# Fewer key pairs in the expert choice, paired low parts in scoring, twelve more row halves moved there, spread loads and a reordered end

## The chip, the cores and the metric

The kernel runs on one core of a Trainium2 chip. The metric is device time in microseconds (us) of one launch, median of 3 runs. The core has a matrix engine (TensorE, PE in the profile, with PEld for its weight loads), a vector engine (VectorE, DVE), a scalar engine (ScalarE, ACT), a third elementwise engine that also issues gathers (GpSimd, POOL) and a queue for loads (SyncE, SP). Each runs its own list of instructions in order; they meet only at semaphores.

## The reference

One layer over 256 tokens of width 2048, in float32:

```python
hn = rmsnorm(x); q, k, v, u, z = split(hn @ w_in)          # 2048 x 5120
x = x + concat(diff_attention(q, k, v), gmlp(u, z)) @ w_out  # 2048 x 2048
xb = rmsnorm(x)
q = (xb @ w_q).reshape(T, 8, 2, 128)                        # 8 heads, two halves
sc = einsum('thcd,hckd->thck', q, sub_keys)                 # 128 keys a half
s1, i1 = top_k(sc[:, :, 0], 16); s2, i2 = top_k(sc[:, :, 1], 16)
best, ci = top_k((s1[..., :, None] + s2[..., None, :]).reshape(T, 8, 256), 16)
idx = 128 * i1[ci // 16] + i2[ci % 16]                      # 16 of 16384 experts
act = gelu(einsum('td,thkd->thk', xb, u_tab[idx]))
x = x + einsum('thk,thkd->td', softmax(best) * act, v_tab[idx])
out = rmsnorm(x)
```

top_k returns its values in falling order. So pair (a, b) has (a+1)(b+1)-1 pairs that are at least as large, and only pairs with (a+1)(b+1) <= 16 can be among the best 16.

## The kernel before, in words

**Stages.** Input projection, attention and gating, output projection, query projection (32 units of `wq_t`), then three stages that the change touches:

- *Scoring* of all 16384 experts for 200 of the tokens: 128 steps `j`, two units a step, `n = 2j` and `2j+1`, from the table `u_t` (512 KB a unit, ring of 6).
- *Values*: 256 units `v` from `peer_v` (512 KB each, ring of 10).
- The *end*: transposes back, residual, final norm, stores.

The other 56 tokens are done by gathering their chosen rows ("halves of rows"): 232 halves of 128x1024 floats (512 KB), each gathered by POOL into one of 3 buffers `PICKED` and used by DVE (`half_rows`: a dot product with x for rows of `peer_u`, L1263, or a multiply-add into an accumulator for rows of `peer_v`, L1271). `HALF_STEPS` says in which scoring steps they are used, `HALF_UNITS` in which units of values. POOL gathers half k when DVE has used half k-3.

**Two-part arithmetic.** Every weight unit is split in a high part that ACT makes (`top(n)`, L737, ring `HI` of 4) and a low part, raw minus high, that DVE makes (`low(n)`, L1205) or, in a few scoring steps, POOL (`by_pool`, L493). In values DVE makes two low parts with one instruction (`low_pair`, L1198).

**Order in scoring.** PE, for unit n: 8 high products of unit n (L1652), then 8 low products of unit n-1 (L1658). DVE in step j: `sum_halves(j)` (waits for PE's low products of unit 2j+1 and for ACT's copy), `low(2j+4)`, `low(2j+5)`, pieces of the choice, `apply_gates`, `one_hots`, `land`, then halves of rows. ACT in step j: `low_half_out(j)` (copies half of the PE result, L762), `top(2j+5)`, `gelu(j)`, `top(2j+6)`, `put_gates`, `gates_into(j+2-SPREAD0)` (waits for DVE's `one_hots` of the same step, L783). From step 37 (`SPREAD0`) to 86 the gates of 4 tokens a step are spread to experts: DVE compares (`one_hots`, L1224), ACT scales (`gates_into`), PE multiplies (`spread`, L1636), DVE and ACT apply.

**The choice** (top 16 of keys, of pairs, and decoding) is a generator of 41 pieces for each of two token tiles. `EARLY` pieces of each tile run in the query stage; `piece_steps` puts the others into scoring steps 1 to 32 by a table of costs and an allowance for each step. A top 16 is five DVE instructions (L1110 to L1114). PE transposes the result of a tile in steps 18 and 34 (L1643). A piece on key half c waits for ACT's copy number c//2+1 of the key scores; in ACT's list copies 1 to 6 stand in the query stage and copy 7 behind the first four `top` of scoring.

**Other loads.** POOL loads `X8` (x rows for the last 24 gathered tokens, five pieces of 192 KB) in one go beside gather 99, and the residual and final gain (twelve pieces of 256 KB) one behind each gather from unit 178 on.

Of the kernel before, what the change touches and what calls it, by code (L numbers as in the profile page):

```python
# [14 lines left out]
P = 128  # L15
T, D = 256, 2048
# [23 lines left out]
RING = 6  # L40
# [31 lines left out]

TILE_ORDER = (1, 0)
EARLY = 12
QUERY_BESIDE = range(WQ0 + 11, WQ_END, 2)
CHOICE0 = 1

def piece_cost(i):  # L80

    if i < HC:
        return 1.55
    if HC + 2 <= i < HC + 2 + PH:
        return 2.35
    return 0.5 if i in (HC + 2 + PH, HC + 2 + PH + 7) else 1.4

def piece_steps():

    steps, j, room = [], CHOICE0, 0.0
    left = [i for o in range(2) for i in range(EARLY, PIECES)]
    while left:
        room += 2.6
        if left[0] in PLAIN and (len(left) < 2 or left[1] in PLAIN):
            room += 0.8
        while left and piece_cost(left[0]) <= room + 0.4:
            room -= piece_cost(left.pop(0))
            steps.append(j)
        j += 1  # L100
    n = PIECES - EARLY
    return [-1] * EARLY + steps[:n] + [-1] * EARLY + steps[n:]
# [5 lines left out]
              for j in range(NKEYS)}  # L108
# [9 lines left out]

HALVES = 4 * NG  # L120
HALF_STEPS = sorted([j for j in range(SPREAD0 - 3, SPREAD_END) if j % 3] + list(range(SPREAD_END, NKEYS - 7))
                    + list(range(SPREAD_END, NKEYS - 7, 4)))
FREE_UNITS = [u for u in range(9, 250) if u not in (NKEYS - 2, NKEYS - 1)]
HALF_UNITS = [FREE_UNITS[i * len(FREE_UNITS) // (HALVES - len(HALF_STEPS))] for i in range(HALVES - len(HALF_STEPS))]
A_DOTS, A_SUMS = 2 * GROUPS_A, 4 * GROUPS_A
B_DOTS, B_SUMS = A_SUMS + 2 * GROUPS_B, A_SUMS + 4 * GROUPS_B
# [8 lines left out]
    return k < B_DOTS, GROUPS_A + (k - A_SUMS) % (2 * GROUPS_B) // 2, k % 2  # L135

X8_AT = len(HALF_STEPS) + 20
SEL_A_AT = 2 * NKEYS - 4
GATHERED = {j: (ROW_SLOTS if j >= ROWS_BACK_AT else 0) + sum(i < j for i in HALF_STEPS) for j in range(NKEYS)}  # L140
S_BANKS = 3
# [24 lines left out]
def hybrid_peer_block(nc, x, w_in, w_out, wq_t, keys_t, u_t, peer_u, peer_v, ws_t, bs_t, gain_t, ffn_gain, z_gain,  # L166
                      final_gain, lambdas, rope, out):
    ctx = ExitStack()
    with ctx:  # L169
# [29 lines left out]

        SC = at("SC", 44 * KB, [P, TT, HC, NKEYS])  # L200
        QTQ = at("QTQ", 60 * KB, [P, HC, T])
        CAND = at("CAND", 60 * KB, [P, PH, TOPK, TOPK])
        EQ = at("EQ", 68 * KB, [P, PH, TOPK, TOPK])
        S16 = at("S16", 84 * KB, [P, TT, HC, TOPK])
        I16 = at("I16", 86 * KB, [P, TT, HC, TOPK], U32)
        I16F = at("I16F", 88 * KB, [P, TT, HC, TOPK])
# [212 lines left out]
        def _(pool):  # L419
# [114 lines left out]
                     for c in range(D // BANK)]  # L534
            for k in range(len(HALF_STEPS) + ROW_SLOTS, HALVES):
                gather(k)
                if k == X8_AT:
                    for r in range(ROWS_B):
                        pool.dma_start(X8[r * NB_:(r + 1) * NB_, :], xg_dram[NA:NS, :]).then_inc(x8_ready, 16)
                if HALF_UNITS[k - ROW_SLOTS - len(HALF_STEPS)] >= NKEYS + 50 and late:  # L540
                    pool.wait_ge(low_used, N_U + NKEYS + 44)
                    dst, src, done = late.pop(0)
                    pool.dma_start(dst, src).then_inc(done, 16)
            assert not late
            pool.wait_ge(fg_ready, 16 * D // BANK)
            for tt in range(TT):
                pool.wait_ge(sums, 7 + 2 * tt + 1)  # L547
                nc.gpsimd.tensor_tensor(X1R[:, tt, 0:HALF], X1R[:, tt, 0:HALF], FG[:, 0:HALF], ALU.mult).then_inc(gained, 1)  # L548

        @block.scalar
        def _(act):
# [297 lines left out]
            def final_scale(tt, cols):  # L850
                act.wait_ge(scaled, tt + 1)
                act.wait_ge(gained, tt + 1)  # L852
                nc.scalar.activation(X1R[:, tt, cols], X1R[:, tt, cols], ACT.Copy, scale=SS[:, 8 + tt:9 + tt])\  # L853
                    .then_inc(act_scaled, 1)

            act.wait_ge(fg_ready, 16 * D // BANK)
# [1 line left out]
            final_squares(0, 1)  # L858
            root(8, SS[:, 6:7])
            final_squares(1, 0)  # L860
            final_squares(1, 1)
# [7 lines left out]
        def _(dve):  # L869
# [246 lines left out]
            def choice(o):  # L1116

                tt = TILE_ORDER[o]
                for c in range(HC):
                    dve.wait_ge(sc_out, c // 2 + 1)  # L1120
                    top16(SC[:, tt, c, :], S16[:, tt, c, :], I16[:, tt, c, :])
                    yield
                dve.wait_ge(sc_out, HC // 2)
                link(v.tensor_copy(I16F[:, tt], I16[:, tt]))
                s1, s2 = S16[:, tt, 0:HC:2, :], S16[:, tt, 1:HC:2, :]
                lists = I16F[:, tt, 0:HC:2, :], I16F[:, tt, 1:HC:2, :]
                heads = [slice(0, PH // 2), slice(PH // 2, PH)]
                for hs in heads:
                    link(v.tensor_tensor(CAND[:, hs], s1[:, hs].unsqueeze(3).broadcast_to(grid),
                                         s2[:, hs].unsqueeze(2).broadcast_to(grid), ALU.add))  # L1130
                    yield
                for h in range(PH):
                    top16(CAND[:, h].rearrange("p a b -> p (a b)"), BEST[:, h], CI[:, h])
# [207 lines left out]
            def add_out(c, tt, count):  # L1341
# [459 lines left out]
```

## Time and profile before

| | us |
|---|---|
| median of 3 runs (lowest, highest) | 1769.67 (1769.17, 1772.12) |
| the profiled execution's own time | 1784.21 |
| its span | 1782.4 |
| PE busy | 1726.1 (97%) |
| DVE busy | 1443.7 (81%) |
| ACT busy | 987.6 (55%) |
| POOL busy | 425.3 (24%) |
| moved by DMA | 483.79 MB, 271 GB/s in the mean |

The profiled execution is 14.5 us longer than the median of the plain ones. Scoring runs from about 458 us to 1122 us of the span, values from there to 1767 us.
### The profile page before, as it was taken

The numbers are of one execution on the slowest core, as the hardware profiler recorded it, in microseconds if no ns is written. First come the engines' busy times: TensorE is split into PE (matmuls) and PEld (weight loads), VectorE is DVE, ScalarE is ACT, GpSimd is POOL, SyncE is SP. The second block draws the span as 40 slices with busy tenths as digits, with TensorE's granted clock in tenths as the row PEclk, the third lists the DMA queues.
The fourth block names the chain that finished last, engine by engine and source line by source line (L and its number), as shares of the span: only waits on it lengthen the run. The fifth ranks groups of instructions, "written<-read, shape, count | busy, mean of one in ns | idle before, by whom it ended". The sixth has DMA issues, their size and how long they took to land. (4 is left out here: it accounts for less than half of the span.)

```text
span 1782.4 us, 28846 instructions
## 1 busy us (share of the span) xinstructions
PE 1726.1 (97%) x10934; PEld 1639.2 (92%) x10934; DVE 1443.7 (81%) x2029; ACT 987.6 (55%) x1600; POOL 425.3 (24%) x324
## 2 busy tenths in 40 slices
PE   8999999999999999999999999997999999999997
PEld 7887778788998899999999999997999989999997
DVE  4546786578799988888989998676998889978996
ACT  5444574444554567777775555554455545554554
POOL 0002300034222001110114454034432323243221
PEclk9999999999999999999999999999999999999999
DMA  7665455676677577777779999899899989999993
GB/s 232 213 186 164 143 156 176 190 258 203 207 225 244 188 238 250 259 249 244 242 242 340 357 370 349 242 351 303 318 366 356 364 307 365 365 358 390 362 362 123
DMA packets 132855, 483.79 MB, mean 271 GB/s; under 512 B 15368, under 2 KB 15522, under 8 KB 132048
## 3 DMA queue, kind: packets, MB, share of 16 engines
q1 hardware_dynamic: 95760, 347.65, 59.3%
q0 software_dynamic: 36672, 133.77, 20.6%
q8 instruction: 87, 1.43, 0.3%
q10 hardware_dynamic: 288, 0.55, 0.1%
q14 instruction: 48, 0.39, 0.1%
HBM read 476.71 MB, written 5.20 MB: 270 GB/s over the span
## 5 line engine op out<-in xcount | busy, mean ns | idle before, releaser
L1692 PE MATMUL PS<-W,HI 128*128 128x400 f32 x2048 | 429.3, 351 | 25.1 <-DVE W L1282 21.5
L737 ACT ACTIVATE HI<-V_RAW 128x1024 fp32r<-128x1024 f32 x256 | 271.5, 1061 | 304.0 <-PE PS L1692 123.4
L1652 PE MATMUL PS<-xT,HI 128*128 128x400 f32 x2048 | 424.4, 349 | 0.1
L1692 PEld LDWEIGHTS PS<-W,HI 128*128 128x128 f32 x2048 | 362.4, 191 | 28.5 <-issue 22.6
L1652 PEld LDWEIGHTS PS<-xT,HI 128*128 128x128 f32 x2048 | 358.0, 190 | 3.0 <-ACT HI L737 1.2
L1198 DVE TENSOR_TENSOR V_LO<-V_RAW,HI 128x2048 fp32r<-128x2048 f32 x128 | 292.8, 2287 | 21.5 <-ACT HI L737 21.2
L737 ACT ACTIVATE HI<-RING_RAW 128x1024 fp32r<-128x1024 f32 x256 | 269.1, 1051 | 64.6 <-DMA RING_RAW<-u_t 59.7
L1205 DVE TENSOR_TENSOR RING_LO<-RING_RAW,HI 128x1024 fp32r<-128x1024 f32 x248 | 292.4, 1218 | 3.2 <-ACT HI L737 3.1
L1658 PEld LDWEIGHTS PS<-xT,RING_LO 128*128 128x128 f32 x2048 | 265.2, 191 | 9.5 <-DVE RING_LO L1205 9.4
L1658 PE MATMUL PS<-xT,RING_LO 128*128 128x200 f32 x2048 | 266.6, 273 | 6.2 <-DVE RING_LO L1205 6.0
L502 POOL DMA_INDIRECT PICKED<-peer_u,PK x116 | 144.1, 1243 | 531.5 <-DVE DOTS L1263 518.8
L1697 PEld LDWEIGHTS PS<-W,V_LO 128*128 128x128 f32 x2048 | 270.0, 192 | 0.0
L1697 PE MATMUL PS<-W,V_LO 128*128 128x200 f32 x2048 | 269.0, 273 | 0.0
L881 DVE TENSOR_TENSOR LO<-RAW,HI 128x1024 fp32r<-128x1024 f32 x121 | 149.4, 1237 | 123.5 <-PE PS L1404 97.6
L502 POOL DMA_INDIRECT PICKED<-peer_v,PK x116 | 167.0, 1439 | 324.0 <-DVE ACC L1271 240.8
L555 ACT ACTIVATE HI<-RAW 128x1024 fp32r<-128x1024 f32 x144 | 152.7, 1065 | 161.8 <-DMA RAW<-wq_t 46.4
L1271 DVE SCALAR_TENSOR_TENSOR ACC<-PICKED,DOTS,ACC 128x1024 f32<-128x1024 f32 (+1 forms) x112 | 143.3, 1281 | 56.4 <-DMA PICKED<-peer_v,PK 55.8
L1263 DVE CUSTOM_DVE_ANT_0 PICKED<-PICKED,X 128x1024 f32<-128x1024 f32 (+1 forms) x116 | 141.2, 1222 | 24.5 <-DMA PICKED<-peer_u,PK 24.2
L1397 PE MATMUL PS<-HI,xT 128*128 128x512 f32 x440 | 139.5, 398 | 2.0 <-ACT xT L580 1.3
L1404 PE MATMUL PS<-HI,xT 128*128 128x512 f32 x440 | 136.2, 391 | 0.6 <-DVE xT L900 0.6
L1404 PEld LDWEIGHTS PS<-HI,xT 128*128 128x128 f32 x440 | 82.5, 188 | 18.4 <-DVE xT L900 1.0
L1397 PEld LDWEIGHTS PS<-HI,xT 128*128 128x128 f32 x440 | 79.7, 188 | 17.2 <-ACT xT L580 1.5
(213 smaller groups left out, 1640.7 us busy)
## 6 DMA issues: line engine op xcount, KB each, us to landing
RING_RAW<-u_t SPq DMA_DIRECT2D x256, 512.0 KB, 4.8
V_RAW<-peer_v SPq DMA_DIRECT2D x256, 512.0 KB, 10.1
RAW<-w_in SPq DMA_DIRECT2D x80, 512.0 KB, 3.8
RAW<-w_out SPq DMA_DIRECT2D x32, 512.0 KB, 4.5
RAW<-wq_t SPq DMA_DIRECT2D x32, 512.0 KB, 4.8
x_spill<-X POOLq DMA_DIRECT2D x2, 1024.0 KB, 5.8
X1R<-x_spill POOLq DMA_DIRECT2D x8, 256.0 KB, 9.4
PICKED<-peer_u,PK POOLq DMA_INDIRECT x116, 8.1
```

The costliest lines, as they stand in the source:

```text
L502: pool.indirect_dma_start(PICKED[k % ROW_SLOTS][:], None, table.rearrange("e (a c) -> (e a) c", a=2), bass.IndirectOffsetOnAxis(PK4[:, hal ...
L555: nc.scalar.activation(HI[:, slot, :], RAW[:, slot, :], ACT.Copy).then_inc(hi_ready, 1)
L737: nc.scalar.activation(HI[:, n % HI_SLOTS, :], raw_of(n), ACT.Copy).then_inc(top_ready, 1)
L881: v.tensor_tensor(LO[:, u % 2, :], RAW[:, u % 4, :], HI[:, u % 4, :].bitcast(FP32), ALU.subtract).then_inc(lo_ready[u % 2], 1)
L1198: nc.vector.tensor_tensor(pair_of(V_LO, v), pair_of(V_RAW, v), HI[:, slot:slot + 2, :].bitcast(FP32), ALU.subtract)\
L1205: v.tensor_tensor(low_of(n), raw_of(n), HI[:, n % HI_SLOTS, :].bitcast(FP32), ALU.subtract).then_inc(low_dve, 1)
L1397: mm(banks[c], high(tt), h[:, halves[c]], start=first, stop=False)
L1404: ins = mm(banks[c], low(tt), h[:, halves[c]], start=False, stop=last and tt > 0)
L1652: return mm(PS[:, j % S_BANKS, 0:2 * ND].rearrange("p (a t) -> p a t", a=2), HI[:, n % HI_SLOTS, kk * P:(kk + 1) * P], xT[:, k, :, 0:ND], ...
L1658: return mm(PS[:, j % S_BANKS, 0:ND], low_of(n)[:, kk * P:(kk + 1) * P], xT[:, k, 0, 0:ND], start=False, stop=k == KT - 1)
L1692: return mm(PS[:, V_BANKS[i], 0:2 * ND].rearrange("p (a t) -> p a t", a=2), HI[:, v % HI_SLOTS, i * P:(i + 1) * P], weights_of(v), start=v ...
L1697: return mm(PS[:, V_BANKS[i], 0:ND], low_of(N_U + v)[:, i * P:(i + 1) * P], weights_of(v)[:, 0, :], start=False, stop=v % NKEYS == NKEYS - 1)
```

## The change

- `CAND`, the sums of the best 16 by 16 keys of a head, shrinks from 256 pairs to 112: the first 4 rows keep 16 columns, the other 12 keep 4. The top 16 of pairs then runs over 112 elements. Decoding a position into row and column takes 9 small instructions instead of 4.
- The piece costs are written anew, the allowance a step falls from 2.6 to 2.1, the first step is 0 instead of 1, and `EARLY` is 13 instead of 12. The steps in which the picks are transposed (18, 34) and `SPREAD0` (37) come out the same. POOL makes 7 low parts instead of 8.
- In every other scoring step DVE makes both low parts with one instruction (`low_two`), which waits for both high parts.
- 91 instead of 79 halves of rows are used in scoring: 3 in 4 steps instead of 2 in 3 while gates are spread, then 1.5 a step instead of 1.25 (steps 87 to 120). The 141 others start at unit 14 instead of 9 of values and leave out units 122 to 129.
- The five `X8` loads go out behind gathers 98, 104, 110, 116 and 122; the twelve late loads behind every third gather.
- The end: POOL multiplies into a new buffer as soon as the residual is added; the last square sum is made in two parts; the mean is partly made ahead.

```diff
-EARLY = 12
+EARLY = 13
-CHOICE0 = 1
+CHOICE0 = 0
+ROOM = 2.1
...
-        room += 2.6
+        room += ROOM
...
-HALF_STEPS = sorted([j for j in range(SPREAD0 - 3, SPREAD_END) if j % 3] + list(range(SPREAD_END, NKEYS - 7))
-                    + list(range(SPREAD_END, NKEYS - 7, 4)))
-FREE_UNITS = [u for u in range(9, 250) if u not in (NKEYS - 2, NKEYS - 1)]
+HALF_STEPS = sorted([j for j in range(SPREAD0 - 3, SPREAD_END) if j % 4] + list(range(SPREAD_END, NKEYS - 7))
+                    + list(range(SPREAD_END, NKEYS - 7, 2)))
+FREE_UNITS = [u for u in range(14, 250) if not NKEYS - 6 <= u < NKEYS + 2]
...
-X8_AT = len(HALF_STEPS) + 20
+X8_AT = range(A_SUMS - 6 * ROWS_B, A_SUMS, 6)
...
-                if HALF_UNITS[k - ROW_SLOTS - len(HALF_STEPS)] >= NKEYS + 50 and late:
+                if HALF_UNITS[k - ROW_SLOTS - len(HALF_STEPS)] >= NKEYS + 50 and late and k % 3 == 0:
...
-                pool.wait_ge(sums, 7 + 2 * tt + 1)
-                nc.gpsimd.tensor_tensor(X1R[:, tt, 0:HALF], X1R[:, tt, 0:HALF], FG[:, 0:HALF], ALU.mult).then_inc(gained, 1)
+                pool.wait_ge(out_added, 4 * tt + 2)
+                nc.gpsimd.tensor_tensor(XG[:, tt, :], X1R[:, tt, 0:HALF], FG[:, 0:HALF], ALU.mult).then_inc(gained, 1)
...
-                for hs in heads:
-                    link(v.tensor_tensor(CAND[:, hs], s1[:, hs].unsqueeze(3).broadcast_to(grid),
-                                         s2[:, hs].unsqueeze(2).broadcast_to(grid), ALU.add))
+                for rows, cols, at0 in ((slice(0, WIDE), TOPK, 0), (slice(WIDE, TOPK), NARROW, WIDE * TOPK)):
+                    shape = [P, PH, rows.stop - rows.start, cols]
+                    link(v.tensor_tensor(CAND[:, :, at0:at0 + shape[2] * cols].rearrange("p h (a b) -> p h a b", b=cols),
...
+            def low_two(n):
+                dve.wait_ge(top_ready, n + 2)
+                ring, slot = n % RING, n % HI_SLOTS
+                v.tensor_tensor(RING_LO[:, ring:ring + 2, :], RING_RAW[:, ring:ring + 2, :],
+                                HI[:, slot:slot + 2, :].bitcast(FP32), ALU.subtract).then_inc(low_dve, 2)
...
-                if j < NKEYS - 2:
+                if j < NKEYS - 2 and not by_pool(2 * j + 5):
+                    low_two(2 * j + 4)
+                elif j < NKEYS - 2:
                     low(2 * j + 4)
-                    low(2 * j + 5)
```

## Rows read from the trace of the kernel before

**Rows 1.** The page, busy time: engine, us, share of the span, instructions.
```profile
PE 1726.1 (97%) x10934; PEld 1639.2 (92%) x10934; DVE 1443.7 (81%) x2029; ACT 987.6 (55%) x1600; POOL 425.3 (24%) x324
```

**Rows 2.** Stretches: from:to, length, busy us (instructions) of each engine, clock, DMA share, GB/s.
```profile
465.00:640.00 175.00, 166.08 (x1109) 163.11 (x1108) 166.61 (x338) 95.58 (x148) 28.77 (x21) 0.99 0.68 216
928.00:1088.00 160.00, 159.40 (x1084) 158.39 (x1083) 146.50 (x213) 91.52 (x145) 74.69 (x41) 1.00 0.95 349
1121.00:1723.00 602.00, 576.92 (x3858) 573.50 (x3858) 508.48 (x454) 309.44 (x368) 196.96 (x162) 0.98 0.98 345
```

**Rows 3.** What PE waited for: us in total, times, longest.
```profile
PE PS L1692 <- DVE W L1282: 21.5, 8, 11.2
PE PS L1658 <- DVE RING_LO L1205: 6.0, 5, 2.3
```

**Rows 4.** Order of time on PE, spreading: start, us, instruction. First, second, last step.
```profile
654.47 1.07 PE L1636 MATMUL PS<-ONE 128*128 128x128 f32 x8
660.06 1.07 PE L1636 MATMUL PS<-ONE 128*128 128x128 f32 x8
...
932.09 1.07 PE L1636 MATMUL PS<-ONE 128*128 128x128 f32 x8
```

**Rows 5.** Order of time on DVE, scoring step 74.
```profile
864.99 0.37 DVE L1214 TENSOR_TENSOR TMP<-PS,HOLES 128x200 f32<-128x200 f32 x1 [0.27 <-issue]
865.27 2.35 DVE L1205 TENSOR_TENSOR RING_LO<-RING_RAW,HI 128x1024 fp32r<-128x1024 f32 x2
867.54 0.46 DVE L1234 TENSOR_TENSOR store<-store,PS 128x296 f32<-128x296 f32 x1
867.91 1.22 DVE L1224 TENSOR_TENSOR ONE<-IOTA,EG 128x1024 f32<-128x1024 f32 x1
```

**Rows 6.** Order of time on ACT, the same step and the next.
```profile
864.58 0.32 ACT L762 ACTIVATE HOLES<-PS 128x200 f32<-128x200 f32 x1
864.79 1.05 ACT L737 ACTIVATE HI<-RING_RAW 128x1024 fp32r<-128x1024 f32 x1
...
869.16 1.28 ACT L783 ACTIVATE ONE<-ONE,EG 128x128 f32<-128x128 f32 x4 [0.78 <-DVE ONE L1224]
870.35 0.32 ACT L762 ACTIVATE HOLES<-PS 128x200 f32<-128x200 f32 x1
```

**Rows 7.** Groups of DVE instructions by shape: busy us, mean ns, idle before.
```profile
L1198 DVE TENSOR_TENSOR V_LO<-V_RAW,HI 128x2048 fp32r<-128x2048 f32 x128 | 292.8, 2287 | 21.5 <-ACT HI L737 21.2
L1110 DVE MAX8 BEST<-CAND 128x8 f32<-128x256 f32 x16 | 6.8, 422 | 0.1
```

**Rows 8.** Order of time where scoring begins, on PE, ACT and DVE.
```profile
460.85 1.04 PE L1658 MATMUL PS<-xT,RING_LO 128*128 128x200 f32 x8
459.18 0.58 ACT L719 ACTIVATE SC<-PS 128x512 f32<-128x512 f32 x1
438.00 0.29 DVE L1110 MAX8 S<-SC 128x8 f32<-128x128 f32 x1
439.70 0.29 DVE L1110 MAX8 S<-SC 128x8 f32<-128x128 f32 x1
458.15 0.69 DVE L1104 TENSOR_REDUCE QTQ<-PS 128x256 f32<-128x512 f32 x1 [3.98 <-PE PS L1423]
```

**Rows 9.** Starts of three steps on DVE; then the gathers of 928 to 1088.
```profile
1009.60 0.36 DVE L1214 TENSOR_TENSOR TMP<-PS,HOLES 128x200 f32<-128x200 f32 x1
1013.57 0.36 DVE L1214 TENSOR_TENSOR TMP<-PS,HOLES 128x200 f32<-128x200 f32 x1
1018.88 0.36 DVE L1214 TENSOR_TENSOR TMP<-PS,HOLES 128x200 f32<-128x200 f32 x1
DMA to landing us min/median/max: 6.7/8.3/10.0
```

**Rows 10.** POOL's five X8 loads in values.
```profile
1225.35 2.58 POOL L539 DMA_DIRECT2D X<-xg_spill  x5
```

**Rows 11.** The last work on ACT.
```profile
1777.43 1.15 ACT L853 ACTIVATE X1R<-X1R,SS 128x1024 f32<-128x1024 f32 x1 [0.92 <-POOL X1R L548]
```

More of the change, by code:

```diff
@@ L65 @@
 WARM = 24
+WIDE = 4
+NARROW = TOPK // WIDE
+PAIRS = WIDE * TOPK + (TOPK - WIDE) * NARROW
 PIECES = HC + 2 + PH + 2 * 7 + 1
@@ L83, in piece_cost @@
         return 1.55
-    if HC + 2 <= i < HC + 2 + PH:
-        return 2.35
-    return 0.5 if i in (HC + 2 + PH, HC + 2 + PH + 7) else 1.4
+    if i < HC + 2 + PH:
+        return 0.8 if i < HC + 2 else 1.65
+    return {HC + 2 + PH: 1.5, HC + 2 + PH + 7: 1.0, PIECES - 1: 1.4}.get(i, 1.25)
 def piece_steps():
@@ L201, in hybrid_peer_block @@
         QTQ = at("QTQ", 60 * KB, [P, HC, T])
-        CAND = at("CAND", 60 * KB, [P, PH, TOPK, TOPK])
+        CAND = at("CAND", 60 * KB, [P, PH, PAIRS])
         EQ = at("EQ", 68 * KB, [P, PH, TOPK, TOPK])
+        PLACE = at("PLACE", 68 * KB, [P, PH, TOPK])
+        START = at("START", 68 * KB + 512, [P, PH, TOPK])
         S16 = at("S16", 84 * KB, [P, TT, HC, TOPK])
@@ L222, in hybrid_peer_block @@
         FJ = at("FJ", 8 * KB, [P, HALF])
+        XG = at("XG", 48 * KB, [P, TT, HALF])
         OUTB = at("OUTB", 12 * KB, [P, DT, T])
@@ L536, in _ @@
                 gather(k)
-                if k == X8_AT:
-                    for r in range(ROWS_B):
-                        pool.dma_start(X8[r * NB_:(r + 1) * NB_, :], xg_dram[NA:NS, :]).then_inc(x8_ready, 16)
-                if HALF_UNITS[k - ROW_SLOTS - len(HALF_STEPS)] >= NKEYS + 50 and late:
+                if k in X8_AT:
+                    r = X8_AT.index(k)
+                    pool.dma_start(X8[r * NB_:(r + 1) * NB_, :], xg_dram[NA:NS, :]).then_inc(x8_ready, 16)
+                if HALF_UNITS[k - ROW_SLOTS - len(HALF_STEPS)] >= NKEYS + 50 and late and k % 3 == 0:
                     pool.wait_ge(low_used, N_U + NKEYS + 44)
@@ L852, in final_scale @@
                 act.wait_ge(gained, tt + 1)
-                nc.scalar.activation(X1R[:, tt, cols], X1R[:, tt, cols], ACT.Copy, scale=SS[:, 8 + tt:9 + tt])\
+                nc.scalar.activation(X1R[:, tt, cols], XG[:, tt, cols], ACT.Copy, scale=SS[:, 8 + tt:9 + tt])\
                     .then_inc(act_scaled, 1)
@@ L860, in _ @@
             final_squares(1, 0)
-            final_squares(1, 1)
+            for c, col in ((2, 3), (3, 10)):
+                act.wait_ge(out_added, 4 + c + 1)
+                squares(X1R[:, 1, c * BANK:(c + 1) * BANK], col, FJ[:, 0:BANK])
             final_scale(0, slice(0, BANK))
@@ L1127, in choice @@
                 heads = [slice(0, PH // 2), slice(PH // 2, PH)]
-                for hs in heads:
-                    link(v.tensor_tensor(CAND[:, hs], s1[:, hs].unsqueeze(3).broadcast_to(grid),
-                                         s2[:, hs].unsqueeze(2).broadcast_to(grid), ALU.add))
+                for rows, cols, at0 in ((slice(0, WIDE), TOPK, 0), (slice(WIDE, TOPK), NARROW, WIDE * TOPK)):
+                    shape = [P, PH, rows.stop - rows.start, cols]
+                    link(v.tensor_tensor(CAND[:, :, at0:at0 + shape[2] * cols].rearrange("p h (a b) -> p h a b", b=cols),
+                                         s1[:, :, rows].unsqueeze(3).broadcast_to(shape),
+                                         s2[:, :, 0:cols].unsqueeze(2).broadcast_to(shape), ALU.add))
                     yield
                 for h in range(PH):
-                    top16(CAND[:, h].rearrange("p a b -> p (a b)"), BEST[:, h], CI[:, h])
+                    top16(CAND[:, h, :], BEST[:, h], CI[:, h])
                     yield
@@ L1141, in choice @@
                     .then_inc(best_ready, 1)
-                for half, (op, by) in enumerate(((ALU.logical_shift_right, 4), (ALU.bitwise_and, 15))):
-                    link(v.tensor_scalar(CIA[:], CI[:], by, None, op))
-                    link(v.tensor_copy(CF[:], CIA[:]))
+                for half in range(2):
+                    if half == 0:
+                        link(v.tensor_scalar(CIA[:], CI[:], 4, None, ALU.logical_shift_right))
+                        link(v.tensor_copy(CF[:], CIA[:]))
+                        link(v.tensor_scalar(CIA[:], CI[:], 2, None, ALU.logical_shift_right))
+                        link(v.tensor_copy(PLACE[:], CIA[:]))
+                        link(v.scalar_tensor_tensor(CF[:], PLACE[:], float(WIDE - WIDE * TOPK // NARROW), CF[:], ALU.add, ALU.max))
+                    else:
+                        link(v.tensor_copy(PLACE[:], CI[:]))
+                        link(v.tensor_scalar(START[:], CF[:], float(NARROW), float(WIDE * (TOPK - NARROW)), ALU.mult, ALU.add))
+                        link(v.scalar_tensor_tensor(START[:], CF[:], float(TOPK), START[:], ALU.mult, ALU.min))
+                        link(v.tensor_tensor(CF[:], PLACE[:], START[:], ALU.subtract))
                     yield
@@ L1345, in add_out, with most_of_mean @@
                     .then_inc(out_added, 1)
+            def most_of_mean(tt):
+                dve.wait_ge(sums, 7 + 2 * tt + 1 + tt)
+                link(v.tensor_scalar(SS[:, 4 + tt:5 + tt], SS[:, tt:tt + 1], 1.0 / D, EPS, ALU.mult, ALU.add))
+                if tt:
+                    link(v.tensor_scalar(SS[:, 5:6], SS[:, 3:4], 1.0 / D, SS[:, 5:6], ALU.mult, ALU.add))
             def final_mean(tt):
-                dve.wait_ge(sums, 7 + 2 * tt + 2)
-                link(v.tensor_scalar(SS[:, 4 + tt:5 + tt], SS[:, tt:tt + 1], SS[:, 2 + tt:3 + tt], None, ALU.add))
-                mean(SS[:, 6 + tt:7 + tt], SS[:, 4 + tt:5 + tt], D)
+                dve.wait_ge(sums, 7 + 2 * tt + 2 + tt)
+                last = SS[:, 10:11] if tt else SS[:, 2:3]
+                v.tensor_scalar(SS[:, 6 + tt:7 + tt], last, 1.0 / D, SS[:, 4 + tt:5 + tt], ALU.mult, ALU.add).then_inc(means, 1)
             def final_inverse(tt):
@@ L1363, in _ @@
                 if i == 5:
+                    most_of_mean(0)
                     final_mean(0)
@@ L1368, in _ @@
             final_scale(0, slice(HALF, D))
+            most_of_mean(1)
             final_mean(1)
```

## The prediction

> **What bounds the kernel now.** I read the busy times first, then busy time by stretch, then what PE waited for, and then the order of time on DVE and ACT inside one step. PE is busy 97% of the span [rows 1], so time can only be won where PE stands still or is made to step slowly, and it is lost wherever something new holds PE. By stretch [rows 2]: in the choice (465 to 640) PE is idle 175.0 - 166.1 = 8.9 us and its clock of 0.99 costs up to 1% of 175, 1.7 us; DVE, busy 95%, is the cause, as the wait for its low parts shows [rows 3]. In the last part of scoring (928 to 1088) PE is idle 0.6 us. In values (1121 to 1723) it is idle 602.0 - 576.9 = 25.1 us, and the clock of 0.98 costs up to 12 more, of which I take 8, since part of the low clock falls into the gaps; 21.5 us of it is the wait for DVE's low parts of the weights, and one of 11.2 us is over half of that [rows 3].
>
> The stage that the busy times hide is the spreading of gates. The reader should compare starts: PE's first two spread groups are 5.59 us apart [rows 4], which is PE's own pace, and from the first to the last (49 steps) it takes 932.09 - 654.47 = 277.6 us where 49 x 5.59 = 273.9. So PE already loses 3.7 us there, at the end of the stage, with no idle time to speak of. What it runs behind is a closed loop of DVE and ACT. One turn, by the starts: ACT copies half of PE's result at 864.58 [rows 6]; DVE adds it (864.99), makes two low parts (865.27), applies gates (867.54), compares (867.91, 1.22 us, so to 869.13) [rows 5]; ACT, which waited for that, scales (869.16) and then copies the next half at 870.35 [rows 6]. The turn is 5.77 us. The halves of rows are not in it: DVE does them while ACT scales.
>
> **The change part by part.**
>
> *Low parts in pairs.* One instruction of 2048 elements takes 2.29 us [rows 7] against 2.35 for two of 1024 [rows 5]: 0.06 saved a step. But it waits for both high parts, and ACT makes the second only after its copy: start 864.79, 1.05 us, done 865.84 [rows 6]. The first of the two single low parts began at 865.27 [rows 5], before the second high part was there. The pair can start at about 865.90, so 0.63 later, and it ends 0.63 - 0.06 = 0.57 later. Everything behind it in the loop (gates, comparison, ACT's scaling, ACT's copy, ACT's high part, the next pair) moves with it, and the next pair waits for ACT again. So the turn becomes 5.77 + 0.57 = 6.34 us late in the stage. Early in the stage it was near PE's 5.59 (it cannot have been much longer, or PE's first steps would show it), and becomes about 6.2. Mean 6.3. Two or three steps of this are taken up by PE's distance to DVE; then PE steps at 6.3. With 46 such steps: 46 x (6.3 - 5.59) = 32.7 us, less the 3.7 lost already: +29 us. Bounds: below, the wait costs nothing and the 3.7 us come back (-4); above, 50 steps at 6.4, 50 x 0.81 - 3.7 = +37. I take +29, because the rows are those of the very loop. Outside the spread ACT doesn't wait for DVE's comparison, the wait delays DVE once and not each turn, and I take 0.
>
> *EARLY 13.* The extra piece of each tile needs ACT's seventh copy of scores, which ends at 459.18 + 0.58 = 459.76 [rows 8]. Today DVE has nothing there: it adds halves at 458.15 and goes on to the low parts. After: two top-16 pieces of 1.70 each (438.00 to 439.70), to 463.2, the addition (0.69 long, 0.61 to the next start), to 463.8, the first low part (1.22), ready at 465.05. PE begins its first low products at 460.85 [rows 8], so it stands for 4.2 us. The gaps in the choice brought a lower clock with them at some places; the same 1.7 here gives +6. Between 0 (if DVE were ahead) and 7.
>
> *Calmer choice.* A top 16 of pairs is five instructions; a MAX8 over 256 takes 0.42 [rows 7], over 128 takes 0.29 [rows 8]. Over 112 I take 0.28: 5 x 0.14 x 8 heads = 5.6 us a tile. The sums over 64 and 48 elements a head instead of 2 x 1024 save about 1.2, five more small decoding instructions cost about 1.3, and the moved piece takes 1.7 out of the stage: 7 us a tile, 14 in all. DVE was over its share in the choice by the 8.9 us that PE stood; 14 less should leave only the steps with two top-16 pieces late. Of 8.9 + 1.7 = 10.6 us I let 1.5 stand: -9. Between -10.6 and, if the new plan is as uneven as the old, -3. POOL makes one low part less (+1.2 us of DVE, inside that).
>
> *Halves in scoring, 91.* While gates are spread they lie beside ACT's scaling: 0. In steps 87 to 120 there are 1.5 a step. DVE: one half makes a step of 1013.57 - 1009.60 = 3.97, two make 1018.88 - 1013.57 = 5.31 [rows 9]; 1.5 make 4.64, just under PE's pace of 5.59 less the spread products (0.83 + a little), 4.7. So DVE's work fits, with no room. The gathers don't quite: a buffer is used, refilled and used again in 2 steps, 9.4 us, at three halves in two steps. Refill takes 8.3 us in the median here, and 6.7 to 10.0 [rows 9], and the use 5.31 - 3.97 = 1.34: 9.6, or 8.0 to 11.3. So a step is lengthened by (9.6 - 9.4)/2 = 0.1 at the median, 0 at the best, 0.97 at the worst; 34 steps: 0, 4, 33 us. With more traffic the refill will not be at today's median, and one late gather now passes through to PE, so I take 0.24 a step: +8.
>
> The traffic asked for is 3.5 x 524288 bytes in 4.7 us, 390 GB/s, and this stretch moved 349 at a DMA share of 0.95 [rows 2]. By its row that is over 100% of what the queues do: 349/0.95 = 367, or 5.0 us a step, +10 for the 34 steps. The Trainium skill (DMA: Bandwidth & Descriptors, Specifications) gives a limit of about 358 GB/s for one core's reads from HBM; by that limit a step would take 5.1 us and the 34 steps +15.
>
> *Values.* 141 halves in place of 153, the first five units later, and none around the flush; X8 no longer as five loads in a row ahead of the next gathers in POOL's list (2.6 us of issue at 1225.35 [rows 10]), to which I put down the longest wait, 11.2 us; the late loads at a third of the density. The gap of 11.2 with its low clock (3) should go, and of the other 19 about a third. 14 + 6 = -20. Between 0 and -30.
>
> *End.* ACT's last scaling waited 0.92 us for POOL [rows 11]; POOL now starts earlier, but DVE's last scaling ends at nearly the same time, and the split square sum costs ACT one more instruction. -0.5, between -1 and +0.5.
>
> **The sum.** +29 + 6 - 9 + 8 - 20 - 0.5 = +13.5, on the profiled execution's own 1784.2 (span 1782.4 plus 1.8 around it): 1797.7. The plain runs are 14.5 us shorter, and the stages that carry work have fixed durations, so most of these 14.5 must be gaps that the profiled execution had and they hadn't; the late gathers of values are the likeliest. What isn't there can't be won: for the plain runs I count the values at -12 instead of -20. 1769.7 + 29 + 6 - 9 + 8 - 12 - 0.5 = 1791.
>
> **The rivals.**
>
> 1. *The pair is not late in the loop* (faster). Place: the loop's turn in steps 39 to 85. Price: -4 instead of +29, total 1791 - 33 = 1758. It decides if ACT's second high part is done before DVE would have begun, that is 0.63 us earlier against DVE than now. For it: PE's distance could let ACT get ahead. Against it: ACT's copy starts right behind its scaling in both turns [rows 6], so ACT has no lead to give, and its list isn't changed. 13%. By it the choice and the values alone carry the result.
> 2. *The gathers or the queues become the bound in steps 87 to 120.* For it: the share of 0.95. Against: DVE's pace can slow PE only until traffic falls again. At the worst refill +33 instead of +8: 1816; at the queue's 367 GB/s about 1793. The case above 1805 has 8%.
> 3. *The gaps bring the clock down.* In the spread stage PE would stand about 0.7 us in each 6.3. For it: the choice, with gaps of up to 2.3 us, has a clock of 0.99 [rows 2, 3]. Against it: the last part of scoring, with idle time in small bits, has 1.00 [rows 2]. If the stage ran at 1.2 GHz, a step of 5.59 would take about 11 and 46 steps +220 us. The Trainium skill (TensorE: Matmul & The Clock Gate, A second HAM failure mode: psum-queue depth-cycling) tells of short idle times between groups that let the clock swing; by it this rival would come true. No row here shows it for gaps under 1 us: 2%.
> 4. *The values gain more than I count* (the full -30) with the loop as forecast: 1773. It counts as the low end of the forecast.
>
> **How the numbers follow.** The forecast (the loop at 6.2 to 6.4, the rest within its bounds) has 75%, rivals 13, 8 and 2%, something else 2%. The forecast's own range is 1777 to 1804. Rival 1 lies outside below; I leave it out and reach to 1773 and 1808. About 0.2% (3.5 us) is what a measurement of this kernel can tell from no change. Slower by more than that: 0.75 less the 2% in which everything goes well, plus 0.08 + 0.02 and half of the rest, 0.84. Faster: rival 1 with 0.13. Within: 0.03.
>
> **What would show it.** In the changed kernel's order of time on DVE each paired low part of steps 38 to 86 starts just behind the end of ACT's second high part, with idle time before it put down to ACT, and PE's spread groups are 6.2 to 6.4 us apart. At the start of scoring PE shows one gap of about 4 us before its first low products. PE's idle time in the choice falls below 3 us; the gap of 11 us in values is gone; DVE waits for gathers in most of steps 87 to 120. The prediction is wrong if spread groups stay within 5.9 us of each other; it is mis-sized if the gathers of steps 87 to 120 land in under 8 us (less), or if values keep gaps of over 20 us (more).

## The result, and the profile after

The changed kernel takes 1799.7 us (median of 4 runs, 1792.7 to 1804.9), the kernel before 1770.8 in the same comparison (1769.2 to 1772.1). The ratio is 1.017, with an interval of 1.015 to 1.020: slower, as forecast, by 28.9 us where 21 were forecast (1791).

The changed kernel's page and its busy times by stretch (from:to, length, PE, PEld, DVE, ACT, POOL, clock, DMA share, GB/s). The stretches are the choice and values, then the spread stage and steps 87 to 122:

```profile
PE 1731.4 (96%) x10934; PEld 1630.4 (91%) x10934; DVE 1431.5 (80%) x1922; ACT 988.2 (55%) x1602; POOL 464.7 (26%) x323
```

```profile
465.00:640.00 175.00, 174.01 (x1170) 172.90 (x1170) 157.90 (x314) 101.76 (x154) 28.44 (x21) 0.98 0.71 224
...
1166.00:1768.00 602.00, 599.54 (x4081) 598.06 (x4080) 523.75 (x463) 325.42 (x386) 207.19 (x155) 1.00 0.97 348
```

```profile
650.00:960.00 310.00, 286.72 (x1967) 270.90 (x1967) 250.51 (x317) 203.56 (x490) 33.83 (x36) 1.00 0.71 229
...
966.00:1143.00 177.00, 165.46 (x1092) 160.19 (x1091) 154.09 (x179) 89.27 (x138) 109.64 (x51) 0.99 0.97 353
```

PE's idle time in the choice is 1.0 us where it was 8.9, in values 2.5 where it was 25.1, and the granted clock in values is 1.00 where it was 0.98 [rows 2]. Steps 87 to 122, where PE was idle 0.6 us in 160, have 11.5 in 177. What PE waited for (us, times, longest) has turned round against [rows 3]: hardly for the weights of values, and 63 times for a paired low part (L1233 is `low_two`, L1227 the single one):

```profile
PE PS L1696 <- DVE RING_LO L1233: 36.3, 63, 1.8
PE PS L1696 <- DVE RING_LO L1227: 4.1, 1, 4.1
...
PE PS L1730 <- DVE W L1311: 2.1, 2, 1.5
```

**The loop of the spread stage.** PE's spread groups, first three and last of 50 (against [rows 4]):

```profile
649.93 1.07 PE L1674 MATMUL PS<-ONE 128*128 128x128 f32 x8
655.52 1.07 PE L1674 MATMUL PS<-ONE 128*128 128x128 f32 x8
661.36 1.07 PE L1674 MATMUL PS<-ONE 128*128 128x128 f32 x8
```

```profile
959.34 1.07 PE L1674 MATMUL PS<-ONE 128*128 128x128 f32 x8
```

The first step is PE's own 5.59; one step later the loop has caught PE. 49 steps take 309.4 us where they took 277.6. One turn on DVE, and on ACT (against [rows 5] and [rows 6]):

```profile
866.40 2.29 DVE L1233 TENSOR_TENSOR RING_LO<-RING_RAW,HI 128x2048 fp32r<-128x2048 f32 x1 [0.59 <-ACT HI L746]
868.61 0.44 DVE L1263 TENSOR_TENSOR store<-store,PS 128x284 f32<-128x284 f32 x1
868.97 1.22 DVE L1253 TENSOR_TENSOR ONE<-IOTA,EG 128x1024 f32<-128x1024 f32 x1
...
871.82 0.37 DVE L1243 TENSOR_TENSOR TMP<-PS,HOLES 128x200 f32<-128x200 f32 x1 [0.28 <-issue]
872.77 2.29 DVE L1233 TENSOR_TENSOR RING_LO<-RING_RAW,HI 128x2048 fp32r<-128x2048 f32 x1 [0.59 <-ACT HI L746]
```

```profile
870.22 1.28 ACT L792 ACTIVATE ONE<-ONE,EG 128x128 f32<-128x128 f32 x4 [0.77 <-DVE ONE L1253]
871.41 0.32 ACT L771 ACTIVATE HOLES<-PS 128x200 f32<-128x200 f32 x1
871.62 1.04 ACT L746 ACTIVATE HI<-RING_RAW 128x1024 fp32r<-128x1024 f32 x1
```

The high part ends at 871.62 + 1.04 = 872.66 and the pair starts at 872.77, after 0.59 us of idle time put down to ACT. A turn is 872.77 - 866.40 = 6.37 us.

**The start of scoring** (against [rows 8]), on ACT, DVE and PE:

```profile
459.38 0.58 ACT L728 ACTIVATE SC<-PS 128x512 f32<-128x512 f32 x1
```

```profile
459.99 0.29 DVE L1121 MAX8 S<-SC 128x8 f32<-128x128 f32 x1 [5.61 <-ACT SC L728]
...
463.40 0.69 DVE L1115 TENSOR_REDUCE QTQ<-PS 128x256 f32<-128x512 f32 x1
464.01 4.62 DVE L1227 TENSOR_TENSOR RING_LO<-RING_RAW,HI 128x1024 fp32r<-128x1024 f32 x4
```

```profile
465.28 2.03 PE L1696 MATMUL PS<-xT,RING_LO 128*128 128x200 f32 x8 [4.07 <-DVE RING_LO L1227]
467.11 1.96 PE L1654 MATMUL PS<-KEYS,QTQ 128*128 128x128 f32 x8
```

DVE stands 5.61 us for the copy of scores, does its two pieces, and PE stands 4.07 us; its next two groups take nearly twice their usual 1.04 and 1.07 us: the lower of the clock's two levels (2.4 and 1.2 GHz).

**Late gathers.** DVE around step 89: two halves in a step, the second waits for its gather:

```profile
977.87 1.22 DVE L1292 CUSTOM_DVE_ANT_0 PICKED<-PICKED,X 128x1024 f32<-128x1024 f32 x1
...
980.56 1.23 DVE L1292 CUSTOM_DVE_ANT_0 PICKED<-PICKED,X 128x1024 f32<-128x1024 f32 x1 [1.47 <-DMA PICKED<-peer_u,PK]
```

What DVE waited for from 966 to 1143 us (us, times, longest):

```profile
DVE ACC L1300 <- DMA PICKED<-peer_v,PK: 12.5, 11, 2.1
DVE PICKED L1292 <- DMA PICKED<-peer_u,PK: 7.9, 6, 2.3
```

These 17 waits lie in 17 of the 34 steps from 87 to 120; in the kernel before 8 of them had one.

**Where the time went**, for the profiled execution of each kernel. The borders of the stages in scoring are the starts of DVE's sums of steps 0, 36, 86 and 122; "values" is PE's first to last low product there. The last columns are the median of the plain runs and its ratio to before, with interval. Each stage is one execution: the four kernels with 91 halves (changed, e1, e4, e6) lie between 185.0 and 191.0 us in steps 86 to 122, so a few us between two of them say little.

| kernel | step 0 at | 0-36 | 36-86 | 86-122 | values | median | ratio |
|---|---|---|---|---|---|---|---|
| before | 465.6 | 183.2 | 284.9 | 167.9 | 640.6 | 1770.8 | |
| changed | 472.6 | 172.3 | 315.7 | 186.1 | 610.7 | 1799.7 | 1.017 (1.015-1.020) |
| e1 single low parts | 471.8 | 171.1 | 285.3 | 185.0 | 608.0 | 1763.4 | 0.9967 (0.9947-0.9988) |
| e2 before + pairs | 464.8 | 182.5 | 316.0 | 172.7 | 623.6 | 1801.5 | 1.018 (1.014-1.023) |
| e3 79 halves | 472.7 | 172.3 | 315.4 | 172.8 | 620.3 | 1794.1 | 1.014 (1.010-1.019) |
| e4 piece later | 465.9 | 171.2 | 315.5 | 190.3 | 607.3 | 1792.6 | 1.014 (1.010-1.018) |
| e5 before + X8 spread | 464.9 | 183.1 | 285.9 | 167.4 | 621.7 | 1764.2 | 0.9977 (0.9963-0.9992) |
| e6 high part ahead | 470.7 | 174.0 | 286.0 | 191.0 | 608.0 | 1771.6 | 1.001 (0.999-1.003) |
| e7 single, later, 79 | 466.0 | 169.9 | 285.0 | 168.5 | 627.6 | 1756.5 | 0.9930 (0.9905-0.9955) |
| e8 single, later, 83 | 467.2 | 169.9 | 284.9 | 167.5 | 614.6 | 1747.4 | 0.9891 (0.9866-0.9915) |
| e9 e8 + pairs, ahead | 466.1 | 172.6 | 285.9 | 170.6 | 615.5 | 1753.3 | 0.9924 (0.9908-0.9939) |
| e10 e8 + pairs outside | 467.1 | 170.6 | 285.5 | 171.9 | 616.4 | 1752.4 | 0.9913 (0.9896-0.9929) |
| e11 before + late loads | 466.2 | 183.1 | 285.2 | 168.9 | 625.5 | 1769.4 | 1.000 (0.999-1.002) |
| e12 e8 + 256 pairs | 465.8 | 180.4 | 286.5 | 168.5 | 613.2 | 1758.1 | 0.9954 (0.9936-0.9971) |

From before to changed, profiled: +7.0, -10.9, +30.8, +18.2, -1.4 (step 122 to the first low product of values), -29.9, +0.5 (behind the last one): +14.3, the difference of the spans. The profiled execution of before was 13.4 us above its plain median, the changed kernel's was not above its own. So I let e11 stand in for the values of before: it is as fast as before in plain runs, was profiled at 1770.6 and has 625.5 us of values. Against that the values gained 14.8 and the sum is 29.4, which fits the 28.9 of the plain runs.

### The profile page after: what moved, and what is told of

Read it like the earlier page. It is cut to its first block and busy times, and to the rows that moved or that the text cites. A ratio compares the mean times of both kernels' runs of the same rounds, so it can differ in the third digit from the quotient of the medians.

```text
span 1796.7 us, 28859 instructions
## 1 busy us (share of the span) xinstructions
PE 1731.4 (96%) x10934; PEld 1630.4 (91%) x10934; DVE 1431.5 (80%) x1922; ACT 988.2 (55%) x1602; POOL 464.7 (26%) x323
## 5 line engine op out<-in xcount | busy, mean ns | idle before, releaser
L1730 PE MATMUL PS<-W,HI 128*128 128x400 f32 x2048 | 424.0, 348 | 2.5 <-DVE W L1311 2.1
L1730 PEld LDWEIGHTS PS<-W,HI 128*128 128x128 f32 x2048 | 358.8, 189 | 4.0 <-issue 2.1
L1696 PE MATMUL PS<-xT,RING_LO 128*128 128x200 f32 x2048 | 273.7, 276 | 40.4 <-DVE RING_LO L1233 36.3
L1233 DVE TENSOR_TENSOR RING_LO<-RING_RAW,HI 128x2048 fp32r<-128x2048 f32 x119 | 272.1, 2287 | 36.5 <-ACT HI L746 35.3
L511 POOL DMA_INDIRECT PICKED<-peer_u,PK x116 | 161.3, 1391 | 527.3 <-DVE DOTS L1292 508.8
L511 POOL DMA_INDIRECT PICKED<-peer_v,PK x116 | 192.5, 1660 | 290.6 <-DVE ACC L1300 259.5
```

The costliest lines, as they stand in the source:

```text
L511: pool.indirect_dma_start(PICKED[k % ROW_SLOTS][:], None, table.rearrange("e (a c) -> (e a) c", a=2), bass.IndirectOffsetOnAxis(PK4[:, hal ...
L1233: v.tensor_tensor(RING_LO[:, ring:ring + 2, :], RING_RAW[:, ring:ring + 2, :], HI[:, slot:slot + 2, :].bitcast(FP32), ALU.subtract).then_i ...
L1696: return mm(PS[:, j % S_BANKS, 0:ND], low_of(n)[:, kk * P:(kk + 1) * P], xT[:, k, 0, 0:ND], start=False, stop=k == KT - 1)
L1730: return mm(PS[:, V_BANKS[i], 0:2 * ND].rearrange("p (a t) -> p a t", a=2), HI[:, v % HI_SLOTS, i * P:(i + 1) * P], weights_of(v), start=v ...
```

## The experiments

The kernel before ran beside each; e1 to e8 ran on one chip, e9 to e12 on another, so across these groups the ratios are to be compared.

**e1, low parts one by one again.**

```diff
-                if j < NKEYS - 2 and not by_pool(2 * j + 5):
-                    low_two(2 * j + 4)
-                elif j < NKEYS - 2:
+                if j < NKEYS - 2:
                     low(2 * j + 4)
+                    low(2 * j + 5)
```

> The changed kernel with the low parts of scoring made one by one again (all else as changed). Theory (the pair waits for ACT's second high part inside the DVE-ACT loop of the spread stage): the spread groups of PE go back from 6.2 to 6.4 us apart to 5.6 to 5.8, the 48 steps from 38 to 86 take about 271 us instead of 303.5, and the total falls by 32 us or a little more (a single low part is ready 1 us sooner, so late gathers in steps 87 to 120 are passed on less): 1765 to 1769. Rival (the stage is slow from more halves of rows, 3 in 4 steps instead of 2 in 3): the stage stays above 295 us and the total above 1790.

1763.4, a little below the forecast range: 36 us less than the changed kernel, and 0.33% faster than before. Steps 36 to 86 fall from 315.7 to 285.3. The denser halves are still there, so they are not what slows the stage. Steps 86 to 122 hardly change (185.0 against 186.1). Pairs are the whole of the slowdown; without them the change is a gain.

**e2, the kernel before with pairs.** The same edit the other way, with `low_two`.

> The kernel before with nothing changed but the low parts of scoring made in pairs. Theory: the same 32 us appear in the spread stage alone, total about 1803; in the choice, where DVE is behind and never waits for ACT, the pair changes less than 2 us. Rival (pairs hurt only together with the extra halves): total within 5 us of before, 1766 to 1776.

1801.5, +32 us. Steps 36 to 86: 284.9 to 316.0. The choice changes by 0.7. But steps 86 to 122 grow from 167.9 to 172.7, which the theory had not said.

**e3, 79 halves in scoring.**

```diff
-... if j % 4] + ... + list(range(SPREAD_END, NKEYS - 7, 2)))
+... if j % 3] + ... + list(range(SPREAD_END, NKEYS - 7, 4)))
```

> The changed kernel with 79 halves of rows in scoring again (2 in 3 steps, then 1.25 a step); the other 153 lie in the units left free by the changed kernel. Theory (three gather buffers turn round too slowly for 1.5 halves a step): steps 86 to 121 take 166 to 171 us instead of 182.4, and the values, with a denser row of gathers, get 3 to 10 us longer: total 1786 to 1796. Rival (the loss in steps 86 to 121 is DVE's own work or the pair's later low part, not the gathers): the stretch stays above 177 us.

1794.1. Steps 86 to 122 fall from 186.1 to 172.8, values rise from 610.7 to 620.3. So, by one profiled execution of each, the twelve halves cost 13 where they went and saved 10 where they came from. The plain medians differ by 5.6 us, and the intervals of the two ratios overlap.

**e4, the thirteenth piece behind the first four low parts.**

```diff
-                if m % 2 == 0 and 0 <= (m - 8) // 2 < EARLY:
+                if m % 2 == 0 and 0 <= (m - 8) // 2 < EARLY - 1:
...
             for n in range(4):
                 low(n)
+            for o in range(TT):
+                next(pieces[o])
+                done[o] += 1
```

> The changed kernel with the thirteenth choice piece of both tiles moved behind DVE's first four low parts of scoring; the plan of all other pieces is unchanged. Theory (PE stands 4.1 us for its first low products because DVE waits for ACT's seventh copy of scores): that gap goes, no gap of over 0.5 us takes its place in the first ten steps, total 5 to 7 us less than the changed kernel, 1793 to 1795. Rival (DVE is then late with the first sum and the gap only moves): total within 2 us of the changed kernel.

1792.6, 7 us less. The intervals of the two ratios overlap, but step 0 starts 6.6 us earlier (465.9 against 472.6), and PE's first low products follow its high ones at once:

```profile
457.20 3.05 PE L1693 MATMUL PS<-xT,HI 128*128 128x400 f32 x16
460.09 1.04 PE L1699 MATMUL PS<-xT,RING_LO 128*128 128x200 f32 x8
```

**e5, the kernel before with X8 spread.** (The gathers are number 98, 104, to 122; the 74 and 80 in the expectation are a slip.)

```diff
-X8_AT = len(HALF_STEPS) + 20
+X8_AT = range(A_SUMS - 6 * ROWS_B, A_SUMS, 6)
```

> The kernel before with one thing changed: the five X8 loads behind gathers 74, 80, ... as in the changed kernel's rule (every sixth gather up to the 122nd) and no longer in a row. Theory (the row of five loads ahead of the next gathers makes the 11.2 us gap of the profiled execution): no gap of over 5 us is left in values, and the plain runs gain 2 to 10 us, 1760 to 1768. Rival (the gap was the profiled execution's own, or the gathers are late anyway): plain runs within 2 us of before.

1764.2 against 1769.0, 0.23% less. The longest wait for the weights in values, 11.2 us in [rows 3] and 7.9 in e11, which has the row of five as well, is gone. First e5, then e11:

```profile
PE PS L1692 <- DVE W L1282: 7.8, 6, 1.9
```

```profile
PE PS L1692 <- DVE W L1282: 13.0, 4, 7.9
```

**e6, the changed kernel with the high part ahead.** On ACT, in steps 35 to 84:

```diff
-                top(2 * j + 5)
+                if not 0 <= j + 1 - SPREAD0 < N_BATCH:
+                    top(2 * j + 5)
...
                 if 0 <= j + 2 - SPREAD0 < N_BATCH:
+                    top(2 * j + 7)
                     gates_into(j + 2 - SPREAD0)
```

> The changed kernel, pairs and all, with one thing changed on ACT: in steps 35 to 84 the high part of unit 2j+7 is made before ACT's gate scaling of step j, where ACT waits for DVE's comparison, and not behind the copy of the next step. Theory (the price of the pair is its wait for that high part inside the loop): the wait goes, a turn is 2.20 + gates + comparison + scaling + copy + sum, 5.6 to 5.8 us, the 48 steps from 38 to 86 take 268 to 273 us instead of 303.5, total 1763 to 1770. Rival (paired low parts are slow by themselves, or release their buffers too late): steps stay above 6.1 us, total above 1790.

1771.6, 1.6 above the forecast range, but 28 us less than the changed kernel with every pair left in. DVE and ACT, one turn:

```profile
862.55 0.37 DVE L1245 TENSOR_TENSOR TMP<-PS,HOLES 128x200 f32<-128x200 f32 x1 [0.32 <-issue]
862.83 2.28 DVE L1235 TENSOR_TENSOR RING_LO<-RING_RAW,HI 128x2048 fp32r<-128x2048 f32 x1
...
868.59 2.28 DVE L1235 TENSOR_TENSOR RING_LO<-RING_RAW,HI 128x2048 fp32r<-128x2048 f32 x1
```

```profile
865.77 1.05 ACT L746 ACTIVATE HI<-RING_RAW 128x1024 fp32r<-128x1024 f32 x1
866.72 1.27 ACT L792 ACTIVATE ONE<-ONE,EG 128x128 f32<-128x128 f32 x4
867.88 0.33 ACT L771 ACTIVATE HOLES<-PS 128x200 f32<-128x200 f32 x1
```

The pair starts right behind the sum, with no idle time, and the turn is 868.59 - 862.83 = 5.76, the 5.77 of before. The high part lies where ACT had waited. This isolates the cause: the same instruction costs 30 us of this stage or nothing, by the order on another engine.

**e7 and e8, the parts that cost undone.** Single low parts (e1), the piece later (e4), and 79 halves (e7), or 83: 3 of 4 steps while spreading, 1.25 a step behind (e8).

> The changed kernel with three parts undone: single low parts, the thirteenth piece behind the first four low parts, 79 halves of rows in scoring. Theory (the three costs add up): 1763.4 of the kernel with single low parts, less 7 for the piece, less 3 to 6 for the halves: 1750 to 1754. Rival (with single low parts a late gather no longer reaches PE, so the 91 halves cost nothing there and moving 12 back only loads the values): 1755 to 1762.

> As the one with three parts undone, but with halves in 3 of 4 steps while gates are spread (they lie beside ACT's scaling) and 1.25 a step behind. Theory (only the density behind the spread stage costs, the denser spread stage is free and takes a few halves from the values): the spread stage is no longer than with 2 in 3, steps 86 to 121 take under 169 us, total 0 to 3 us less than with 79 halves: 1748 to 1753. Rival (one more half in twelve steps costs in the spread stage too): total 1 us or more above the one with 79.

1756.5 and 1747.4. e7 missed its forecast of 1750 to 1754 by 2.5, and its total lies in the rival's range, though the rival's reason doesn't hold: against e1, steps 86 to 122 are 16.5 us shorter (168.5 against 185.0), so with single low parts too the 91 halves cost there; but values are 19.6 us longer (627.6 against 608.0). e8 came out 9 us below e7, where 0 to 3 were forecast, and the difference lies in values (614.6 against 627.6). It is the fastest kernel of the study, 1.1% faster than before. In e8 steps 930 to 1089 keep PE busy at a DMA share of 0.98:

```profile
930.00:1089.00 159.00, 158.95 (x1085) 158.77 (x1084) 147.28 (x205) 91.03 (x138) 75.13 (x43) 1.00 0.98 364
```

The four more halves in the spread stage are free there (284.9 against 285.0).

**e9, e8 with pairs and the high part ahead; e10, e8 with pairs outside steps 35 to 87.**

> The fastest kernel so far (single low parts, piece later, 83 halves; 1747.4) with pairs back and ACT's high part made ahead in the spread stage. Theory (made ahead, the high part costs the pair nothing, and the pair saves 0.06 to 0.1 a step): spread groups from first to last in 276 to 281 us, total 1745 to 1751. Rival (pairs cost outside the spread stage as well, because a late gather reaches PE sooner): total 1753 or more.

> The same fastest kernel with pairs only outside steps 35 to 87. Theory (outside the loop ACT doesn't wait for DVE's comparison, so the pair's wait is not repeated): within 2 us of 1747.4, the choice and the steps behind the spread stage within 2 us of those with single low parts. Rival (a pair hands the first low part over 1 us later, which costs wherever DVE is behind): 1751 to 1758.

Both theories missed, and the totals lie where the rivals put them: ratios 0.9924 and 0.9913 against 0.9891, some 4 to 6 us more than e8. Their intervals overlap that of e8, so the totals alone don't prove it, but the stages agree: steps 86 to 122 take 170.6 and 171.9 us in place of 167.5, and e3 against e7, the same halves with and without pairs, 172.8 and 168.5. Where DVE isn't behind, the pair waits there too, as in e10:

```profile
1001.03 0.36 DVE L1243 TENSOR_TENSOR TMP<-PS,HOLES 128x200 f32<-128x200 f32 x1
1002.17 2.29 DVE L1233 TENSOR_TENSOR RING_LO<-RING_RAW,HI 128x2048 fp32r<-128x2048 f32 x1 [0.78 <-ACT HI L746]
```

That wait did not reach PE. PE waited five times in these steps of e10, 2.6 us in all, each time for a paired low part, and in e8 never. The longest of the five began with a load of `u_t` that came late. ACT waited for it to make the second high part, the pair waited for ACT, and PE for the first low part, whose own high part had been there since 958.98 us:

```profile
962.41 1.06 ACT L746 ACTIVATE HI<-RING_RAW 128x1024 fp32r<-128x1024 f32 x1 [2.93 <-DMA RING_RAW<-u_t]
963.57 2.29 DVE L1233 TENSOR_TENSOR RING_LO<-RING_RAW,HI 128x2048 fp32r<-128x2048 f32 x1 [2.44 <-ACT HI L746]
965.92 1.14 PE L1700 MATMUL PS<-xT,RING_LO 128*128 128x200 f32 x8 [0.66 <-DVE RING_LO L1233]
```

The pair has one more effect there, on gathers. POOL's gather instruction takes 0.94 us at the least. When it starts 0.07 or 0.08 us behind a low part, it ends 0.8 us after that part does: with pairs it then takes 3.02 us, with single ones mostly 1.96. In the changed kernel 22 of the 51 gathers of 966 to 1143 us took 3.02 or 3.03. First the changed kernel, then e8:

```profile
1098.96 3.03 POOL L511 DMA_INDIRECT PICKED<-peer_v,PK  x1 [0.92 <-DVE ACC L1300]
1098.88 2.28 DVE L1233 TENSOR_TENSOR RING_LO<-RING_RAW,HI 128x2048 fp32r<-128x2048 f32 x1
```

```profile
1049.08 1.95 POOL L511 DMA_INDIRECT PICKED<-peer_v,PK  x1 [1.05 <-DVE ACC L1300]
1049.01 2.35 DVE L1227 TENSOR_TENSOR RING_LO<-RING_RAW,HI 128x1024 fp32r<-128x1024 f32 x2
```

How much of the 3 to 5 us is due to late inputs of the pair and how much to gathers issued 1.06 us later was not tried one by one.

**e11, the kernel before with only the late loads spread.** The edit is `and late and k % 3 == 0`.

> The kernel before with only the twelve late loads (residual and final gain) behind every third gather. Theory (they crowd the gathers of units 180 to 200): the gaps of over 1 us of PE behind 1580 us go, and the plain runs gain 1 to 5 us, 1764 to 1768. Rival (three buffers decide, not these loads): within 1 us of before.

1769.4 against 1769.6: nothing, as the rival said. Spreading those loads alone gains nothing.

**e12, e8 with 256 pairs and the old decoding.**

> The same fastest kernel with 256 pairs a head and the old decoding, in the new plan of pieces. Theory (the 112 pairs take about 11 us of DVE's work out of the choice and that is what ends PE's gaps there): steps 0 to 36 take 178 to 183 us instead of 169.9, total 8 to 13 us more, 1755 to 1760. Rival (the new plan and the early start do it): steps 0 to 36 under 174 us, total within 4 us of 1747.4.

Ratio 0.9954 against 0.9891, 11 us more. Steps 0 to 36: 180.4 against 169.9, with PE's gaps of the choice back:

```profile
PE PS L1687 <- DVE RING_LO L1216: 6.8, 4, 2.3
```

## Why the prediction was right, point by point

- **The turn of the loop**: forecast 6.34, measured 6.37, because the duration of each link stood in the rows and ACT's list fixed their order. The stage cost 30.8 us where 29 were forecast. e1, e2 and e6 each show it: the part undone, done alone, and made harmless.
- **Pairs outside the spread stage**: forecast 0, measured 3 to 5 us in steps 86 to 122 with 79 or 83 halves (e2, e9, e10, and e3 against e7). With 91 halves it can't be told well: 186.1 to 191.0 with pairs, 185.0 in e1. This is the step that failed: "the wait delays DVE once and not each turn". It holds where DVE is behind (the choice: 182.5 against 183.2). Behind the spread stage DVE is sometimes level with PE, and then any late second high part holds up the first low part too, as the rows of e10 show.
- **EARLY 13**: forecast a gap of 4.2 and 6 in all, measured 4.07 and 7.0 (e4: 7).
- **The choice**: forecast -9, measured -10.9. A MAX8 over 112 pairs takes 0.273 to 0.278 us, where 0.28 was taken. e12 puts the gain on the pairs and not on the plan.
- **91 halves**: forecast +8, too small. With pairs they cost 13.3 us (e3), with single low parts 16.5 (e7 against e1). The recorded 0.24 us a step was a guess above the 0.1 of its rows. 51 halves in the 177 us of steps 87 to 122 are three in 10.4 us, where 9.4 were wanted and 9.6 was the median turn of a buffer; that turn was taken from rows with single low parts, where a gather instruction is up to 1.06 us shorter (see e10). Rival 2's other form, the queues' own limit, is not excluded: at the 364 GB/s that e8 moves in the same steps with PE busy, the 3.5 x 524288 bytes of a step take 5.04 us, 12 more than before over 34 steps (an estimate). The changed kernel's steps 87 to 120 take 5.24 in the mean, and the stretch moved 353 GB/s at a share of 0.97. e1 has the shorter gather instructions and is still only 1.1 us faster in steps 86 to 122, which speaks for the queues. The Trainium skill's limit of about 358 GB/s (DMA: Bandwidth & Descriptors, Specifications) is near both numbers, but e8 is above it, so the measured 364 decides. Three buffers that come round too late and full queues both fit the waits for gathers; no run changed the number of buffers alone, so this stays open.
- **Values**: forecast -20 on the profiled execution and -12 in plain runs, measured -29.9 and about -15. X8 in a row was worth 4.8 us of plain time (e5), the late loads nothing (e11). Fewer halves are most of the rest: e3, which differs from the changed kernel only in where its halves lie, has 9.6 us more of values, and e8 has 6.6 more than e1 with 8 more halves. The later first one and the free units at the flush were not tried one by one.
- **The end**: forecast -0.5, the profiled executions show +0.5, inside what they can tell.
- **Rival 1** (the pair is not late) is refuted by the rows of the turn. **Rival 3** (the clock falls in the spread stage): PE stood 23.3 us of 310 there, 0.5 a step, and the granted clock of that stretch is 1.00; the gap of 4.07 us did bring the lower level, the small ones didn't. What the Trainium skill says of short idle times (TensorE: Matmul & The Clock Gate, A second HAM failure mode: psum-queue depth-cycling) was not seen at gaps of this size.

Two of the signs that the prediction names came out otherwise or can't be read: DVE waited for gathers in half of steps 87 to 120, not in most, and the changed kernel's trace has no landing times of gathers (there medians are 8.7 and 8.5 us in e10, with pairs, and 8.1 and 8.4 in e8).

The forecast was 9 us short of the measured time: +2 from the loop, +1 from the start, -2 from the choice, +10 from steps 86 to 122, -3 from the values, and 1 because the kernel before ran at 1770.8 in this comparison and not at 1769.7. That the choice and the values came out better than forecast hid part of the miss in steps 86 to 122, so the total came nearer than its worst term partly by luck. How the +10 divides can't be said: taking back the halves wins 13 of the stretch's 18 us, taking back the pairs alone wins 1.

## What to carry to other kernels

Merging two instructions saved 0.06 us here, but the merged one waits for the later of its inputs: find which engine makes that input, what that engine does just before, and whether the chain closes on itself; in a closed loop the wait is paid at every turn, and no busy time shows it. Such a loop is found by comparing starts of the same instruction one turn apart, on the bound engine and on the others. Work moved into a stage must be held against the turn of its buffers, and against the best rate that the queues have shown in such a stretch, and not only against the engine's share.

## What the runs showed that was not expected

- The time of values seems steep in the number of halves there: 153 in 228 units take 627.6 us (e7) or 620.3 (e3), 149 take 614.6 (e8), 141 take 608.0 (e1); in plain runs e7 and e8 differ by 9 us, with intervals that overlap a little. The four halves alone would be 5 us of DVE's time, which isn't the bound. e7 and e3 have the same halves and differ by 7.3 us, so part of it is scatter. Why it is so steep wasn't settled.
- ACT's wait for loads of `peer_v` fell from 83.6 us to 15.2 in values (first before, then changed; us, times, longest), though the loads are the same and the stretch moves 348 GB/s against 345:

```profile
ACT HI L737 <- DMA V_RAW<-peer_v: 83.6, 75, 2.4
```

```profile
ACT HI L746 <- DMA V_RAW<-peer_v: 15.2, 18, 1.3
```
